# Joint modulation sums: the second vector's term by ScalarE and GpSimd instead of VectorE

## What is computed

```python
sc = jax.nn.silu(c)
sc_ctx = jax.nn.silu(c_ctx)
for l in range(DEPTH_2):
    shift, scale, gate = jnp.split(sc @ w_ada[l] + b_ada[l], 3, axis=-1)
    shift_c, scale_c, gate_c = jnp.split(sc_ctx @ w_ada[l] + b_ada[l], 3, axis=-1)
    h_lat = rms_norm(x, norm_g[l]) * (1.0 + scale[:, None]) + shift[:, None]
    h_ctx = rms_norm(xc, norm_g[l]) * (1.0 + scale_c) + shift_c
    ...
```

## Time and profile before

| | |
|---|---|
| median of 3 runs | 3426.2 us (3422.11 to 3426.39) |
| profiled execution, its own time | 3418.37 us |
| its span | 3416.6 us |
| busy: PE, PEld, DVE, ACT, POOL | 90%, 74%, 64%, 36%, 4% |
| mean granted TensorE clock | 0.949 of full speed |
| moved by DMA | 589.24 MB, mean 172 GB/s |

### The profile page before, as it was taken

One profiled execution on the slowest core, in us unless ns is written; L12 is line 12 of the kernel. 1 busy time (PEld: TensorE's weight loads), 2 busy tenths in 40 slices (PEclk: granted clock), 3 DMA queues, 4 the chain that ended last, 5 costly groups with the idle time before them and its releaser, 6 DMA issues. The chain is left out here.

```text
span 3416.6 us, 42406 instructions
## 1 busy us (share of the span) xinstructions
PE 3068.3 (90%) x16441; PEld 2545.0 (74%) x16441; DVE 2197.8 (64%) x3206; ACT 1217.1 (36%) x1825; POOL 140.2 (4%) x202
## 2 busy tenths in 40 slices
PE   5999789897889999999998999888899879978898
PEld 2587558886779999998887888766767668956666
DVE  4767645748767778787865677945346755594345
ACT  6631324413344443434343222124243123224343
POOL 1000000001000000000001000000000000000000
PEclk9999999998999999999999999989999989989999
DMA  7876024641657667667873556520305544652324
GB/s 261 283 254 230 22 82 154 228 173 32 212 195 249 226 229 235 227 216 272 272 267 115 185 172 192 179 92 31 105 1 191 184 138 163 213 181 96 111 68 160
DMA packets 255577, 589.24 MB, mean 172 GB/s; under 512 B 21977, under 2 KB 30401, under 8 KB 251024
## 3 DMA queue, kind: packets, MB, share of 16 engines
q1 hardware_dynamic: 246336, 546.64, 48.7%
q0 software_dynamic: 8640, 39.22, 3.2%
q10 hardware_dynamic: 400, 0.66, 0.1%
HBM read 571.72 MB, written 14.72 MB: 172 GB/s over the span
## 5 line engine op out<-in xcount | busy, mean ns | idle before, releaser
L2488 ACT ACTIVATE w_hi<-raw 128x1024 fp32r<-128x1024 f32 (+1 forms) x732 | 742.5, 1032 | 1245.0 <-PE bank L2559 639.8
L2509 DVE TENSOR_TENSOR w_lo<-raw,w_hi 128x1024 fp32r<-128x1024 f32 (+1 forms) x732 | 859.3, 1191 | 463.2 <-ACT w_hi L2488 459.0
L652 DVE SCALAR_TENSOR_TENSOR acc<-raw,sc_t,acc 128x1024 f32<-128x1024 f32 x480 | 601.5, 1281 | 54.4 <-DMA acc<-in_b_ada 46.3
L2557 PE MATMUL bank<-w_hi,l_hT_hi 128*128 128x512 f32 (+1 forms) x1056 | 399.6, 378 | 43.5 <-DVE w_lo L2509 43.5
L2567 PE MATMUL bank<-f_hT_hi,w_hi 128*128 128x256 f32 x1408 | 405.8, 288 | 29.0 <-DVE w_lo L2509 29.0
L2568 PE MATMUL bank<-f_hT_lo,w_hi 128*128 128x256 f32 x1408 | 403.6, 287 | 0.0
L2569 PE MATMUL bank<-f_hT_hi,w_lo 128*128 128x256 f32 x1408 | 403.4, 287 | 0.0
L2558 PE MATMUL bank<-w_lo,l_hT_hi 128*128 128x512 f32 (+1 forms) x1056 | 395.0, 374 | 0.0
L2559 PE MATMUL bank<-w_hi,l_hT_lo 128*128 128x512 f32 (+1 forms) x1056 | 394.8, 374 | 0.0
L2567 PEld LDWEIGHTS bank<-f_hT_hi,w_hi 128*128 128x128 f32 x1408 | 275.4, 196 | 33.3 <-DVE w_lo L2509 31.6
L2569 PEld LDWEIGHTS bank<-f_hT_hi,w_lo 128*128 128x128 f32 x1408 | 275.5, 196 | 0.0
(11 more groups left out here) (437 smaller groups left out, 4677.1 us busy)
## 6 DMA issues: line engine op xcount, KB each, us to landing
raw<-in_w_in SPq DMA_DIRECT2D x240, 512.0 KB, 4.8
raw<-in_w_mod SPq DMA_DIRECT2D x192, 512.0 KB, 5.2
raw<-in_w_ada SPq DMA_DIRECT2D x192, 512.0 KB, 4.5
raw<-in_w_up SPq DMA_DIRECT2D x176, 512.0 KB, 5.3
raw<-in_w_out SPq DMA_DIRECT2D x96, 512.0 KB, 4.7
raw<-in_w_down SPq DMA_DIRECT2D x88, 512.0 KB, 5.2
raw<-in_w_in SPq DMA_DIRECT2D x32, 288.0 KB, 3.2
raw<-in_w_ukv SPq DMA_DIRECT2D x16, 512.0 KB, 4.5
```

The source lines that it names most:

```text
L652: e.scalar_tensor_tensor(acc[a][:, :], raw[s % RAW_SLOTS][:, :], scalar, acc[a][:, :], ALU.mult, ALU.add).then_inc(fma_done, 1)
L2488: e.activation(slot(w_hi[u % SPLIT_SLOTS], g.width), slot(raw[s % RAW_SLOTS], g.width), ACT.Copy).then_inc(hi_ready, 1)
L2509: e.tensor_tensor(slot(w_lo[u % SPLIT_SLOTS], g.width), slot(raw[s % RAW_SLOTS], g.width), slot(w_hi[u % SPLIT_SLOTS], g.width).bitcast(F3 ...
L2557: e.matmul(o, xh[:, k, tok], hi[:, kk, :], start=first, stop=False)
```

## The change

In a joint step DVE now makes only the first vector's update. ACT then multiplies the whole buffer in place with the second vector's scalars (`ctx_scale`, line 666 of the changed kernel), after DVE's update is done, and POOL adds the buffer to the second accumulator (`ctx_add`, line 676). The buffer is free only after POOL's add. ACT does not scale at the hosted step itself: it keeps a list and works it off behind the `w_hi` of the next unit. PE's turn waits for both accumulators. In the output projection the two groups of 16 steps are also hosted elsewhere: with `lead=9` they stood behind units 9 to 14 and 19 to 24, and with the new `hosts` they stand behind units 4 to 15 and 20 to 29 (of 32). Single-vector groups are as before.

```diff
                 if g.kind == "F":
-                    counted["fma"] += 1 + g.both
+                    counted["fma"] += 1
                     g.fmas.append(counted["fma"])
-                    slot_free.append((fma_done, counted["fma"]))
+                    if g.both:
+                        counted["ctx"] += 1
+                        g.ctx_adds.append(counted["ctx"])
+                        slot_free.append((ctx_added, counted["ctx"]))
+                    else:
+                        slot_free.append((fma_done, counted["fma"]))
...
                 def fma(e, g, j, mine=mine, inits=inits):
                     s = g.slots[j]
                     e.wait_ge(raw_landed[s % RAW_SLOTS], 16 * (s // RAW_SLOTS + 1))
+                    a = mine[0]
                     if j == 0:
-                        for a in mine:
-                            e.wait_ge(acc_ready[a], 16 * inits[a])
+                        e.wait_ge(acc_ready[a], 16 * inits[a])
                     else:
                         e.wait_ge(fma_done, g.fmas[j - 1])
-                    for n, a in enumerate(mine):
-                        scalar = sc_t[:, 32 * pair + 16 * n + j:32 * pair + 16 * n + j + 1]
-                        e.scalar_tensor_tensor(acc[a][:, :], raw[s % RAW_SLOTS][:, :], scalar, acc[a][:, :],
-                                               ALU.mult, ALU.add).then_inc(fma_done, 1)
+                    scalar = sc_t[:, 32 * pair + j:32 * pair + j + 1]
+                    e.scalar_tensor_tensor(acc[a][:, :], raw[s % RAW_SLOTS][:, :], scalar, acc[a][:, :],
+                                           ALU.mult, ALU.add).then_inc(fma_done, 1)
+
+                def ctx_scale(e, g, j):
+                    e.wait_ge(fma_done, g.fmas[j])
+                    r = raw[g.slots[j] % RAW_SLOTS]
+                    e.activation(r[:, :], r[:, :], ACT.Copy,
+                                 scale=sc_t[:, 32 * pair + 16 + j:32 * pair + 17 + j]).then_inc(ctx_scaled, 1)
+
+                def ctx_add(e, g, j, mine=mine, inits=inits):
+                    a = mine[1]
+                    if j == 0:
+                        e.wait_ge(acc_ready[a], 16 * inits[a])
+                    else:
+                        e.wait_ge(ctx_added, g.ctx_adds[j - 1])
+                    e.wait_ge(ctx_scaled, g.ctx_adds[j])
+                    e.tensor_tensor(acc[a][:, :], acc[a][:, :], raw[g.slots[j] % RAW_SLOTS][:, :],
+                                    ALU.add).then_inc(ctx_added, 1)
 
                 def pe(e, g, mine=mine):
                     e.wait_ge(fma_done, g.fmas[-1])
+                    if both:
+                        e.wait_ge(ctx_added, g.ctx_adds[-1])
...
-                gemms(gs, sums_l1[1], lead=9, hooks=join, ready=ready_cat)
+                gemms(gs, sums_l1[1], hosts=[(4, 12), (20, 10)], hooks=join, ready=ready_cat)
...
+                if who == "act":
+                    if g is None or g.kind != "F":
+                        for f, n in scales:
+                            f.ctx_scale(e, f, n)
+                        scales = []
+                    elif g.both:
+                        scales.append((g, j))
...
+                    if at < len(phase.steps) and phase.steps[at][0].both:
+                        g, j = phase.steps[at]
+                        g.ctx_add(e, g, j)
```

More of the change, by code:

```diff
@@ L105, in __init__ @@
         self.fmas = []
+        self.ctx_adds = []
         self.both, self.fma, self.prefill = 0, None, None
+        self.ctx_scale = self.ctx_add = None
         self.turn_at = 0
@@ L219, in build @@
         fma_done = sem("fma_done")
+        ctx_scaled = sem("ctx_scaled")
+        ctx_added = sem("ctx_added")
         acc_zero = sem("acc_zero")
@@ L312, in stage @@
             program.append(("stage", (early, ready, fill), engines))
-        counted = {"main": 0, "slot": 0, "unit": 0, "fma": 0, "sum": 0, "group": 0, "mod": 0}
+        counted = {"main": 0, "slot": 0, "unit": 0, "fma": 0, "ctx": 0, "sum": 0, "group": 0, "mod": 0}
         slot_free = []
@@ L702, in sum_groups @@
                 g = Group("F", w, KT, col, FMA_W, (), pair, None, dve, pe, pool, store if row is not None else None)
-                g.both, g.fma = both, fma
+                g.both, g.fma, g.ctx_scale, g.ctx_add = both, fma, ctx_scale, ctx_add
                 g.prefill = prefill if gain is not None else None
```

## The result

The changed kernel takes 3483.1 us (median of 4 runs, 3480.4 to 3484.0), the kernel before 3426.3 us (4 runs, 3422.1 to 3426.7). The ratio is 1.0167 with a 95% interval of 1.0154 to 1.0179: 57 us slower. The forecast was 3465 us, with 3395 to 3512 as its range. So the direction and the main mechanism held, and the size was 18 us short.

A forecast was written before the change was run, and what follows sets the result against it. The prediction took PE as the limit over the span and DVE in the joint groups' bursts. Its terms, 7 + 11 + 0 + 25 - 4 = +39 us, on 3426 gave 3465 us, range 3395 to 3512.

The forecast's parts named there:

- What bounds the kernel: Whole span: PE the limit; DVE the limit in up bursts, late input and output projection, just fast enough in down.
- The first two input groups: Input projection, first two joint groups: 4.1 us of DVE excess against 16.2 us of finished units, so 0.
- Exclusion between POOL's addition and DVE: Joint steps: two-SBUF-input operations exclude each other; DVE occupied or kept out 3.51 us instead of 2.39, 18.0 us more per group.
- +7, +11, 0 and +25 together, and -4: Forecast changes in us: up +7, down +11, input first two groups 0 and last two +25, output -4.
- the 10 us that I took off for the convolution: Up projection: convolution operations reading PSUM and one SBUF tensor run beside POOL, about 10 us overlap: 17.1 - 10 = +7.
- 22.5 us of old waiting against 19 of new: Output projection: PE waiting of 5 and 14 us, together 19 instead of 22.5, giving -4.
- I cost the scaling at nothing: Joint groups: ACT has room for the scalings, 1.03 us each, 16.5 us per group, so they add nothing.
- price for a lost cover: Joint groups: if ACT's spare time no longer covered the scalings, they would cost 16.5 us per group.
- The first (no exclusion): Rival, chance 0.15: additions run beside DVE; up 8, input 14, output 17, together 39 us less, 3387 us.
- The second (absorbed): Rival, chance 0.23: exclusion mostly hidden by waits and reserves; up 0, down +4, input +10, output -14, about 3426 us.
- The third (the ring): Rival, chance 0.20: buffers held longer make the buffer ring the limit in up and down, +80 us, about 3500.
- The rival's other sign: Changed profile under the buffer-ring rival, chance 0.20: ACT waits for loads, besides SP waiting for POOL's additions.

The follow-up runs named there:

- the new places alone: The kernel before with only the new hosting of the two output projection groups, DVE making both updates: 3401.0 us, ratio 0.9926.
- the memsets: The changed kernel with each POOL addition replaced by three clearings that write SBUF but read nothing, second sums left out: 3382.9 us, ratio 0.9875.
- the scaling alone: The changed kernel without POOL's additions: ACT scales, the buffer is free after the scaling, second sums left out: 3374.5 us.
- the memset ahead of the addition: The changed kernel without ACT's scaling, with a 0.96 us clearing on POOL ahead of each addition: 3452.7 us.

## Why the prediction came out as it did

**What bounds the kernel: right.** DVE was the limit in the bursts of the joint groups, and each place that was named as tight became longer (the output projection against the new places alone, 425.2 to 408.8 us). The first two input groups, named as free, stayed free of waits but for 2.5 us (windows of the changed kernel, first and second, then the late ones):

```profile
1909.80:1988.50 78.70, 78.70 (x349) 65.17 (x348) 63.91 (x36) 31.58 (x34) 46.35 (x15) 1.00 0.54 174
2004.60:2077.40 72.80, 70.29 (x368) 60.80 (x366) 63.44 (x33) 29.05 (x32) 45.77 (x16) 1.00 0.50 156
2091.30:2165.30 74.00, 61.11 (x310) 52.47 (x309) 73.28 (x49) 27.75 (x29) 44.25 (x15) 0.93 0.54 172
2199.30:2296.70 97.40, 72.39 (x286) 57.24 (x285) 95.52 (x125) 30.58 (x31) 46.60 (x17) 0.89 0.52 167
```

In the last two PE idles 12.9 and 25.0 us, against 4.9 and 14.8 in the earlier trace rows, and the waits from 2085 to 2300 put all of it down to `w_lo`:

```profile
PE bank L2594 <- DVE w_lo L2543: 37.9, 15, 10.6
```

**Exclusion between POOL's addition and DVE: right**, shown by the memsets and the means of the groups. The premise that every addition keeps DVE out for its whole length was too high. Without additions DVE's four busy times fall from 970 to 789 us, with them they are 1062. So the additions lengthened DVE's operations by 273 us, 27 us per group (1.71 per addition) and not 37.1 (2.32). Net of the removed updates DVE is busy 9 us longer per group, not 18.0. The rest of the exclusion fell on POOL, whose additions took 2.85 us instead of 2.32, and on times in which DVE had to wait anyway or read PSUM.

**The terms of the sum.** Without the scaling the chip gave +10.7, +11.9, +22.9 and -11.1 for the forecast's +7, +11, 0 and +25 together, and -4. So these terms were sized well. In up, the 10 us that I took off for the convolution are 7.1 us of its operations (lines 1402 and 1405) under an addition without the scaling, and only 1.6 us in the changed kernel. In output I had weighed 22.5 us of old waiting against 19 of new. The new places alone gave 24 us in that stretch (432.8 to 408.8), of which 8.6 are PE's own busy time, a term that the forecast lacked, and the additions took 12.9 back (421.7).

**The step that failed: "I cost the scaling at nothing".** ACT had room by its busy time, and the sum needed its latency. The scaling stands between DVE's update and the next `w_hi`, in a chain that goes back to DVE. With the additions it costs 30 us (3483.1 against 3453.6), of which 13.3 are in the up and 6.6 in the down stretch. Of the 13.3 us PE waited 6.0, the other 7.3 are its own busy time at a clock of 0.90 instead of 0.94. The prediction's own price for a lost cover, 16.5 us per group, would have made 165 us, so most of it was still covered. The two errors partly cancel. Without the scaling the chip stands at +27 us by the medians (+34 by the spans, since the profiled execution of before was 8 us below its median) against the forecast's +39, and the 30 us of the scaling turn 12 too many into 18 too few. That the forecast came within 18 us is in part luck.

**The rivals.** The first (no exclusion) is what the memsets and the scaling alone show: 3374.5 to 3382.9 us against its 3387. Its total was near and its premise wrong. Its terms were less near: with scaling alone the four stretches are 3.0, 0.1, 23.9 and 21.1 us shorter, against its 8, 0, 14 and 17. The second (absorbed) fell: its reserves hid little, but its remark on the places was the better half of it. The third (the ring) has its signature in the trace, SP waiting for POOL's additions at both of its DMA lines:

```profile
SPq L2498 <- POOL acc L676: 401.0, 71, 27.4
SPq L2502 <- POOL acc L676: 391.6, 89, 16.1
```

Yet in the kernel with the memsets SP waits 347.1 and 319.0 us for POOL at the same two lines, and it is 100 us faster. In the kernel before SP waited 383.3 and 322.9 us for DVE's updates. And a mean hold longer by 2.2 us (the memset ahead of the addition) cost nothing by the median. So most of this is SP standing at a full ring, and no limit. The rival's other sign, ACT waiting for loads, didn't come either: 97.3 us for those of the input projection, where it was 186.5. The ring comes into play, as I read it, only when the hold grows by a whole unit.

## What to carry to other kernels

Before work is moved off a busy engine, ask which of its operations the new one shuts out: 160 additions on POOL lengthened DVE by 273 us, more than the 181 us by which the updates that they replaced had kept it busy. An engine with idle time is no free host if the moved operation stands between two steps of the limiting engine's chain: cost its latency there, and cost it again after the other effects of the change have used up the slack. Where a burst makes an engine the limit for 60 us at a time, spreading the same work over more units gave 52 us without moving any of it to another engine.

## What the runs showed of the hardware

**A wait of PE costs more than its length.** In the kernel before, in the output projection, PE waited 6.29 us for a `w_lo` and started again at 2710.39. The windows around it:

```profile
2701.60:2704.10 2.50, 2.50 (x12) 1.73 (x10) 2.43 (x2) 0.00 (x0) 0.00 (x0) 1.00 0.00 0
2710.40:2714.70 4.30, 4.30 (x10) 3.43 (x11) 4.20 (x4) 0.00 (x0) 0.00 (x0) 0.50 0.84 263
2714.70:2718.00 3.30, 3.30 (x15) 2.46 (x14) 3.20 (x4) 1.06 (x1) 0.00 (x0) 1.00 0.76 237
```

The granted clock is 1.00 (2.4 GHz) ahead of the wait, 0.50 (1.2 GHz) for 4.3 us behind it, and 1.00 again. In those 4.3 us 10 matmuls started, in the 3.3 us after them 15. In the up projection of the changed kernel this was nearly half of the loss: +12.9 us of PE's idle time and +11.1 us of busy time for the same matmuls, at a clock of 0.90 instead of 0.96. Some 3 us of it are within what the stretch varies by.

**The exclusion goes both ways, and isn't always paid.** An addition of 2.32 us cost DVE 1.71 us of busy time on average and took 2.85 us itself. Half an addition cost DVE 0.64 us and the kernel a fifth of a whole one (21 against 109 us). Memsets on POOL of the same length, which write SBUF and read nothing, cost DVE's operations nothing (1191 and 1281 ns, as before).
